# RWKV stream: tile steps on four array quarters, one eviction per pair, bonus sums a slot later, and an order table per engine

## The reference, cut to what matters

```
def step(S, xs):                       # S: 64 x 64 per head
    w_t, kk_t, a_t, k_t, v_t, r_t = xs
    sa = jnp.einsum('bhvk,bhk->bhv', S, kk_t)
    S = S * w_t[:, :, None, :] - sa[..., None] * (kk_t * a_t)[:, :, None, :] + v_t[..., None] * k_t[:, :, None, :]
    y = jnp.einsum('bhvk,bhk->bhv', S, r_t)
...
w_log = -softplus(-(w0[d] + tanh(wl) @ w2[d])) - 0.5     # decay: a low-rank product
a     = sigmoid(a0[d] + al @ a2[d])                      # rate: another
bonus = (sum(r * k_fwd * r_k) + sum(r * k_bwd * r_k)) * v
out   = (group_norm(y) + bonus) * (sigmoid(gl) @ g_up)
```

## Time and profile before

| | |
|---|---|
| median of 3 runs | 3592.82 us (3590.53 to 3599.41) |
| the profiled execution | 3589.35 us, its span 3587.5 us |
| mean granted TensorE clock | 0.954 |
| PE | 3217.4 us busy (90%), 33804 matmuls |
| DVE | 1638.1 us (46%) |
| ACT | 722.9 us (20%) |
| POOL | 888.6 us (25%) |

### The profile page before, as it was taken

The page is one execution under the profiler, slowest core; times in us unless marked ns, Lnnn a source line. Parts: engine busy times, 40 slices in busy tenths (PEclk is TensorE's granted clock), DMA queues, the critical chain, the costliest instruction groups (busy, mean ns, idle before and its releaser), DMA issues. The chain is left out here.

```text
span 3587.5 us, 76386 instructions
## 1 busy us (share of the span) xinstructions
PE 3217.4 (90%) x33804; PEld 2696.0 (75%) x33804; DVE 1638.1 (46%) x2670; ACT 722.9 (20%) x1286; POOL 888.6 (25%) x465
## 2 busy tenths in 40 slices
PE   5888999999999999998879677777876999999999
PEld 4654878888888887887768577767775878888887
DVE  4062443443443447021534466766765543343444
ACT  4011220100110103011222343443431210101100
POOL 3103232322322332331110000000004334334432
PEclk9999999999999999998889798999997999999999
DMA  5455001111111110222010211010102011111112
GB/s 217 166 189 194 30 30 36 36 42 36 36 42 36 36 36 31 99 80 88 1 51 0 68 30 34 27 36 27 35 9 102 30 47 48 53 41 53 47 41 77
DMA packets 73787, 207.61 MB, mean 58 GB/s; under 512 B 9745, under 2 KB 28817, under 8 KB 73234
## 3 DMA queue, kind: packets, MB, share of 16 engines
q1 hardware_dynamic: 70034, 188.55, 15.6%
q10 hardware_dynamic: 3456, 14.55, 1.0%
HBM read 182.22 MB, written 20.84 MB: 57 GB/s over the span
## 5 line engine op out<-in xcount | busy, mean ns | idle before, releaser
L155 POOL TENSOR_TENSOR w_hi<-w_raw,zero 128x1024 fp32r<-128x1024 f32 x158 | 304.0, 1924 | 1262.5 <-PE ps L167 803.7
L167 PE MATMUL ps<-u_hi,w_hi 128*128 128x512 f32 (+1 forms) x2232 | 601.6, 369 | 14.6 <-POOL w_lo L158 9.1
L167 PE MATMUL ps<-u_lo,w_hi 128*128 128x512 f32 (+1 forms) x2232 | 600.0, 368 | 0.0
L167 PE MATMUL ps<-u_hi,w_lo 128*128 128x512 f32 (+1 forms) x2232 | 599.4, 368 | 0.0
L787 DVE SCALAR_TENSOR_TENSOR ffn_cv<-ps,small,ffn_cv 128x1023 f32<-128x1023 f32 (+1 forms) x132 | 134.1, 1016 | 769.6 <-ACT ffn_cv L1138 768.1
L167 PEld LDWEIGHTS ps<-u_hi,w_hi 128*128 128x128 f32 x2232 | 386.7, 188 | 95.8 <-issue 16.1
L167 PEld LDWEIGHTS ps<-u_lo,w_hi 128*128 128x128 f32 x2232 | 387.1, 188 | 73.1
L167 PEld LDWEIGHTS ps<-u_hi,w_lo 128*128 128x128 f32 x2232 | 386.9, 188 | 73.0
L158 POOL TENSOR_TENSOR w_lo<-w_raw,w_hi 128x1024 fp32r<-128x1024 f32 x158 | 383.2, 2425 | 12.4
L1138 ACT ACTIVATE ffn_cv<-ps,small 128x1280 f32<-128x1280 f32 (+1 forms) x88 | 107.8, 1225 | 1238.1 <-PE ps L167 1226.6
L631 DVE SCALAR_TENSOR_TENSOR h<-ps,mod,h 128x1024 f32<-128x1024 f32 x210 | 206.6, 1013 | 138.8 <-PE ps L1087 138.4
(11 more groups left out here) (381 smaller groups left out, 5447.5 us busy)
## 6 DMA issues: line engine op xcount, KB each, us to landing
w_raw<-in_ffn SPq DMA_DIRECT2D x132, 512.0 KB, 3.5
ada_ring_t<-in_ada SPq DMA_DIRECT2D x20, 512.0 KB, 6.0
w_raw<-in_cd_in SPq DMA_DIRECT2D x20, 512.0 KB, 4.0
z_scratch<-cd_stage ACTq DMA_DIRECT2D x15, 640.0 KB, 5.5
ada_ring<-in_ada SPq DMA_DIRECT2D x18, 512.0 KB, 6.5
ada_first<-in_ada SPq DMA_DIRECT2D x16, 512.0 KB, 15.5
ada_ring_s<-in_ada SPq DMA_DIRECT2D x14, 512.0 KB, 5.0
ada_ring_w<-in_ada SPq DMA_DIRECT2D x14, 512.0 KB, 6.7
```

The lines of the kernel that those rows point to most:

```text
L155: pool.tensor_tensor(hi, K.raw[:, raw, :], K.zero[:, 0:1].to_broadcast([P, KT * P]), ALU.add).then_inc(self.hi_done, 1)
L167: mm = pe.matmul(K.ps[:, slot, c, 0:width], wt[:, s, w], x[:, k, at:at + width], start=start and n == 0, stop=stop and n == 2)
```

## The change

- The first P step, the first XT product, the Z products and the W product read and write different halves, through new `flip`, `*_at` and `az_at`. For this the n=0 step lays half of its turned inputs the other way and n=2 has four more matmuls. The Z products and their copy move from n=3 to the last level (n=12).
- The low-rank inputs wl and al are loaded once, in the two halves of one buffer; the products use four quarters, with one result in B2 and the other in B1. The gate product is one matmul of all 128 rows.
- n=4, 6, 8, 10: ACT copies the whole pair, DVE nothing.
- The mask product has 768 columns, rw_c and rw_cx are made by one backward and one forward scan and one subtraction, rw_ar by two products in place of four.
- Low-rank products in r = 0 and 2, sums in r = 1, bonus in r = 8; the variance step of a tail one slot earlier.
- Slots are run by `PE_ORDER`, `ACT_ORDER` and `DVE_ORDER`: N, M, O are the newest, middle and oldest tile; b the work through B1, r that through B2; q, l, s, k, d, g, c pieces of ACT's group work; p, f `prepare` and `finish`.

```diff
-    def tile_at(k, s):
-        for i in range(s, TILES, NS):
-            if 0 <= k - GAP * i < STAGES:
-                return i, k - GAP * i
-        return None
+    def tile_at(k, age):
+        i = k // GAP - age
+        return (i, k % GAP + GAP * age) if 0 <= i < TILES else None
...
+    LORA, SUMS, SPREAD, GATE, BONUS = (0, 2), 1, 4, 6, 8
...
+    AGES = "NMO"
+    PE_ORDER = ["OrMbN", "OMbrN", "rbOMN", "brMON", "rbMON",
+                "bONrM", "bONrM", "bOMrN", "brMON", "MbONr"]
+    ACT_ORDER = ["OlcdgMskqN", "OqkNsMgldc", "slcdNOkqMg", "cMNOqldkgs", "cdOgqNsMlk",
+                 "lMOcdgskqN", "NqMOkgsldc", "slcdNkqOMg", "kcMgNqOlds", "dcgqNOMlks"]
+    DVE_ORDER = ["fMpbON", "ObpfMN", "ObMfpN", "MObfpN", "MbOfpN",
+                 "bpfNMO", "OfMbNp", "MbNfpO", "MObNfp", "MbOfpN"]
...
     def flip(j, h, d):
-        return 0 if j == 0 else h ^ d if j % 2 else h
+        return d if j == 0 else h ^ d if j % 2 else h
...
+    def az_at(h, d):
+        return 2 * (h ^ d) + h
...
-                for q in range(2):
-                    sp.dma_start(R.wl[HALF[q], b, :], K.z[18][0:64, cols]).then_inc(kwa_in[b], 16)
-                    sp.dma_start(R.al[HALF[q], b, :], K.z[18][64:128, cols]).then_inc(kwa_in[b], 16)
+                sp.dma_start(R.wal[:, b, :], K.z[18][:, cols]).then_inc(kwa_in[b], 16)
...
+                    if latent_group(g):
+                        sp.wait_ge(b1_read, bonus_read(g))
                     load_v(g + 3)
...
+                        for part, side in ((0, 0), (1, 1), (0, 1), (1, 0)):
+                            to = (B2[:, 0:256], B1[:, 256:512])[part]
+                            mm = pe.matmul(to[SIDE[side], :], R.mats[SIDE[part], g // 5, way, 64 * side:64 * side + 64],
+                                           R.wal[SIDE[part], g % 2, :], start=True, stop=True)
...
+                        mm = pe.matmul(B2[:, 0:256], R.mats[:, g // 5, 2, :], R.gl[:, g % 2, :], start=True, stop=True)
...
+                    for c, hp in both:
+                        mm = pe.matmul(bank(s, hp)[HALF[1 - c], 128:192], ar[HALF[hp], 1, 0, HALF[c]],
+                                       R.beta[HALF[hp], g % 3, 1, toks(c)], start=True, stop=True)
...
+                    if j == LV - 1:
+                        for h, d, c in quarters(lambda h, d: h ^ d):
+                            mm = pe.matmul(block(s, 2, az_at(h, d))[HALF[c ^ h ^ d]], SS[HALF[c], s, h, 1, d, :],
+                                           TM[HALF[c], s, 4, HALF[h]], start=True, stop=True)
...
-                    for u, (h, d) in enumerate(HD):
-                        for c in range(2):
-                            mm = pe.matmul(b0[HALF[c], u * P:(u + 1) * P], XT[HALF[c], s, xt_at(LV, h, d), :],
-                                           AZ[HALF[c], s, u, :], start=True, stop=True)
+                    for h, d, c in quarters(lambda h, d: h ^ d):
+                        q = HALF[c ^ h ^ d]
+                        mm = pe.matmul(bank(s, h ^ d)[HALF[c], h * P:(h + 1) * P], XT[q, s, xt_at(LV, h, d), :],
+                                       AZ[q, s, az_at(h, d), :], start=True, stop=True)
...
-                        act.copy(R.XX[:, s, :, 0:2, :].rearrange("p k i c -> p k (i c)"),
-                                 b0[:, 128:384].rearrange("p (k c) -> p k c", k=2)).then_inc(low_out[s], 1)
+                    if j < LV - 1:
+                        act.copy(R.XX[:, s].rearrange("p k (b i) c -> p b k (i c)", b=2),
+                                 banks(s)[:, :, 128:384].rearrange("p b (k c) -> p b k c", k=2)).then_inc(x_out[s], 1)
...
-                elif 3 <= n < 3 + 2 * (LV - 1):
-                    j = (n - 4) // 2
-                    dve.wait_ge(sq_done[s], LV * turn + j + 1)
-                        ins = dve.tensor_copy(R.XX[:, s, :, 2:4, :].rearrange("p k i c -> p k (i c)"),
-                                              b1[:, 128:384].rearrange("p (k c) -> p k c", k=2))
...
             for k in range(FIRST, LAST):
-                if tile_at(k, 0) is not None:
-                    tile_step(k, 0)
-                background(k)
+                for what in PE_ORDER[k % 10]:
+                    if what in AGES:
+                        if tile_at(k, AGES.index(what)) is not None:
+                            tile_step(k, AGES.index(what))
+                    elif what == "b":
+                        background(k)
+                    else:
+                        rows(k)
```

More of the change, by code:

```diff
@@ L1927, in __init__ @@
         self.bp = keep("bp", [P, 256])
-        self.one = keep("one", [P, 256])
+        self.one = keep("one", [P, 2, 256])
         self.yc = keep("yc", [P, 256])
@@ L1931, in __init__ @@
         self.z = keep("z", [P, 2, 256])
-        self.mask = keep("mask", [P, 2, 2, CL])
+        self.mask = keep("mask", [P, 3, 2, CL])
         self.level = keep("level", [P, 6, 2, CL])
-        self.mats = keep("mats", [P, PAIRS, 6, CL])
+        self.mats = keep("mats", [P, PAIRS, 3, P])
         self.vec = keep("vec", [P, PAIRS, 10])
@@ L2094, in b2_after, with lora_before, bonus_read @@
         return B2_USED[k] + 1
+    def lora_before(k):
+        slots = [slot_of(g, r) for g in range(RGROUPS) for r in LORA]
+        return max([x for x in slots if x < k], default=None)
     def spread_read(g):
-        return b1_after(10 * g - 6)
+        return b1_after(slot_of(g, SPREAD))
     def sums_read(g):
-        return b2_after(10 * g - 8)
+        return b2_after(slot_of(g, SUMS))
+    def bonus_read(g):
+        return b1_after(slot_of(g, BONUS))
     def gate_read(g):
@@ L2330, in background, with rows @@
                     mm.then_inc(b1_ready, 1)
+            def rows(k):
+                g, r = prep(k)
                 if uses_b2(k):
                     pe.wait_ge(b2_read, B2_USED[k])
-                    if g is not None and r < 2:
-                        pe.wait_ge(kwa_in[g % 2], 80 * (g // 2 + 1))
+                    if g is not None and r in LORA:
+                        way = LORA.index(r)
+                        pe.wait_ge(kwa_in[g % 2], 32 * (g // 2 + 1))
                         pe.wait_ge(const_in, 32)
[L2336 to L2340, removed]
+                        pe.wait_ge(b1_read, B1_USED[k])
+                        for part, side in ((0, 0), (1, 1), (0, 1), (1, 0)):
+                            to = (B2[:, 0:256], B1[:, 256:512])[part]
+                            mm = pe.matmul(to[SIDE[side], :], R.mats[SIDE[part], g // 5, way, 64 * side:64 * side + 64],
+                                           R.wal[SIDE[part], g % 2, :], start=True, stop=True)
+                    if g is not None and r == SUMS:
                         pe.wait_ge(kk2_done, g + 1)
@@ L2352, in background, with tile_step @@
                                                start=True, stop=True)
[L2353 removed]
+                    if g is not None and r == GATE and latent_group(g):
                         n = sum(1 for x in range(g % 2, g + 1, 2) if latent_group(x))
[L2355 to L2359 removed]
+                        pe.wait_ge(gl_in[g % 2], 16 * n)
+                        mm = pe.matmul(B2[:, 0:256], R.mats[:, g // 5, 2, :], R.gl[:, g % 2, :], start=True, stop=True)
                     mm.then_inc(b2_ready, 1)
[L2362 to L2364 removed]
+            def tile_step(k, age):
+                i, n = tile_at(k, age)
+                s, turn, t = i % NS, i // NS, token_tile(i)
                 g, tl = i // 2, t % 2
@@ L2580, in _ @@
             for k in range(FIRST, LAST):
-                if tile_at(k, 0) is not None:
-                    tile_step(k, 0)
-                background(k)
-                for s in (1, 2):
-                    if tile_at(k, s) is not None:
-                        tile_step(k, s)
+                for what in ACT_ORDER[k % 10]:
+                    if what in AGES:
+                        if tile_at(k, AGES.index(what)) is not None:
+                            tile_step(k, AGES.index(what))
+                    elif what == "q":
+                        squares(k)
+                    elif what == "l":
+                        lora(k)
+                    elif what == "s":
+                        sums(k)
+                    elif what == "k":
+                        keys(k)
+                    elif what == "d":
+                        decays(k)
+                    elif what == "g":
+                        gates(k)
+                    else:
+                        centred(k)
         @engines.vector
@@ L2937, in _constants @@
         before = src < dst if way == 0 else src > dst
-        mask[:, way, 0] = before
-        mask[:, way, 1] = before | (src == dst)
+        mask[:, 1, way] = before
+        mask[:, 0, way] = mask[:, 2, way] = before | (src == dst)
         for i in range(6):
```

280 lines of the change are left out of this document (133 added, 147 removed).

## The result

The changed kernel takes 3531.03 us (median of 4 runs, 3528.01 to 3538.58), the kernel before on the same chip 3592.66: ratio 0.9828, 95% interval 0.9808 to 0.9849. That is 61.6 us less; 112 were forecast.

A forecast was written before the change was run, and what follows sets the result against it. It took PE as nearest its limit, the bonus-sum wait as largest hole. Terms sum to -5.6 us per ten-slot period (33.7 to 28.1); times 19.5, plus 3 at the start, 112 us less: 3481, own range 3455 to 3512, 8 in 10 3428 to 3550.

The forecast's parts named there:

- Four quarters and clock: RWKV stream, PE: rearranged steps, low-rank and gate products on four array quarters, -3.3 us per period; fewer low-clock windows, -0.5.
- Bonus sum: Stream, bonus sums moved to slot 8: PE's wait for DVE's rw_bp shrinks, -1.4 us per period (ends 0 and -2.4).
- DVE, one eviction, order tables: Stream, per period: less DVE work -0.4 us, pair copies by ACT alone +0.3, each engine's own slot order -0.6.
- Issue: PE's instruction issue in the stream: the same instructions in less time, +0.3 us per period (ends -0.3 and +1.5).
- rival A: Stream: engines come apart, period 26.1 us, PE busy plus issue with no waits left; 3442 us, chance 0.2.
- issue gaps over 5 us per period: Sign in the changed kernel's profile: PE issue gaps exceeding 5 us per period would show the forecast wrong.
- Start: Kernel start: fewer input loads let the first product begin earlier, first group's low-clock products are halved; -3 us once.
- B: Stream: saved PE time turns to waits, slots with heavy DVE work set the length, period near 31; 3537 us, chance 0.2.
- C: Stream: ScalarE's single queue becomes the path, pair copies start late behind group work; slower, 3617 us, chance 0.06.

The follow-up runs named there:

- The wider columns: Changed kernel with each XT product of the five levels streaming its 64 moving columns twice, the copy unread, no TensorE instruction more: 3535.83 us, ratio 0.9839.

## Why the prediction was right and wrong

The direction held, and the time lies in the range of 8 in 10 (3428 to 3550), but above the forecast's own range of 3455 to 3512; of the size, 62 of 112 us came. By its own steps, per period:

- **Four quarters and clock, -3.8 forecast, -3.4 measured in PE's busy time.** The paces were right: the W step 0.44 us for 0.9, four low-rank products 0.46 us (2344.83 to 2345.29) for 0.86; the clock went from 0.94 to 0.99. What was wrong is that I let this busy time count in full to the end. The wider columns put about half of it back with no change of the time clear of the measurement.
- **Bonus sum, -1.4 forecast.** The wait went from 43.2 us to 0.2, -2.4, the upper end. Alone, it gave the kernel before 19 to 21 us (27 forecast).
- **DVE, one eviction, order tables: -0.4, +0.3, -0.6 forecast, together -0.7.** The waits for the two engines fell by 0.75, so the sum is right, by luck: its parts are not. The single eviction isn't a cost but worth 26 us in this kernel, 1.3 per period with the other sign. The rule of the Trainium skill that I weighed ("TensorEngine Tiling (Array Packing)", Performance Considerations, "PSUM Bottleneck", use both engines for the eviction) goes the wrong way here: with both, +26 us. VectorE, busy 19.5 us per period, was the scarcer of the two; ScalarE was busy 15.0.
- **Issue, +0.3 forecast, +3.0 measured. This is the step that failed.** I had the row, 143 packets of 16 KB in the stretch, one in 4.2 us, and took the rate for PE's appetite and the gaps for a cost that stays. I never asked how fast packets can come. They come 3.80 to 3.82 us apart on average in the six kernels in which little else is waited for, so my 28.1 us (3.5 per packet) and rival A's 26.1 (3.3) lay below the 30.5 that 8.0 packets take. The saved array time turned into issue gaps. The warning stood in the text all the same: issue gaps over 5 us per period.
- **Start, -3 forecast.** PE's first wait for the inputs went from 12.36 to 11.7 us, 0.7. The 18 periods and this leave 2 us for the slots around them.
- **Rivals.** B's number, 3537, is nearest, but not its cause: waits for VectorE's and ScalarE's answers fell. Only its raised issue term was right in kind, and three times too small. A would need every packet at the shortest spacing seen; C is excluded by the 143 us for which ScalarE stands idle before its pair copies.

With the packets' pace in place of the busy time, 8.0 x 3.81 = 30.5 against 33.7 give -3.2 x 19.5 = -63 us, the measured change. This is no test, since the 3.81 come from the changed kernel itself; the tests are the runs above. At this pace the way from 4.25 to 3.81 us per packet was all there was to win without taking instructions away.

Open: what starts a packet's transfer 1.24 us after PE has run on, what the 1.39 us behind its landing are, and what the clock in the run with 64 x 128 weights fell for.

## What to carry to other kernels

Count instructions beside array time. Where an engine runs hundreds of small instructions in a few microseconds and its gaps have no releaser, divide the stretch by its instruction packets; if that comes near the mean of 3.8 us that stood here, look for fewer and wider instructions first: saved array time turned into gaps here, though a busier VectorE still cost time (+26 us). Wider moving columns cost nothing here; wider weights (64 x 128) cost more array time than the instructions they saved. Two products with the same weights make one matmul if their moving blocks lie at one stride, and which engine should evict is read from who is waited for.

## What the runs showed of the hardware

- TensorE's small matmuls were supplied at one packet of 256 instructions in 3.80 to 3.82 us (about 67 per us) in the changed kernel and five of its variants, with PE busy 411 to 440 us in stretches of 527 to 587. The packet's transfer is 1.1 us of that; 1.39 us after its landing PE ran on, 1.24 us later the next transfer began.
- 64 x 64 matmuls keep a pace by the quarters that a step uses, not by their order: 8 of 128 columns in 0.44 us either way (the changed kernel and the run with two quarters at a time).
- Matmuls with 64 x 128 weights ran in pairs, one in each row half, but a pair took 0.11 us for 64 columns, where four records of 64 x 64 weights on four quarters took 0.058 us; going over to 64 x 64 weights took 0.20 us from start to start, back 0.15.
- GpSimd's power took 161 ns a column (41.2 us for 256, in the run without the small sums), its multiply of the same shape 0.61 us (in the run that lays the factors on a diagonal).
